# Value products ahead of the weight turns in every attention round

## The reference, cut to what matters

```
s = einsum('bchd,bkhd->bhck', q, k) * scale      # scores
s = where(allowed, s, -inf)
p = softmax(s, axis=-1)                          # weights
o = einsum('bhck,bkhd->bchd', p, v)              # value products
```

## Time and profile before

| | |
|---|---|
| median of the runs | 2584.94 us |
| the profiled execution | 2582.44 us |
| its span (first to last instruction) | 2580.6 us |
| PE busy | 2462.2 us, 95% of the span |
| DVE busy | 1743.6 us, 68% |
| ACT busy | 1078.4 us, 42% |
| mean granted TensorE clock | 0.987 of full speed |
| share of PE in the chain that ended last | 62% |

### The profile page before, as it was taken

One profiled execution on the slowest core, in us unless ns is written; L12 is line 12 of the kernel. 1 busy time (PEld: TensorE's weight loads), 2 busy tenths in 40 slices (PEclk: granted clock), 3 DMA queues, 4 the chain that ended last, 5 costly groups with the idle time before them and its releaser, 6 DMA issues.

```text
span 2580.6 us, 34583 instructions
## 1 busy us (share of the span) xinstructions
PE 2462.2 (95%) x13194; PEld 2051.7 (80%) x13194; DVE 1743.6 (68%) x2562; ACT 1078.4 (42%) x1846; POOL 361.4 (14%) x413
## 2 busy tenths in 40 slices
PE   3999999999999999999989999999999999999998
PEld 3678987779988878877648887888888888777997
DVE  6977886857995776776865474666575665345454
ACT  3466554556554212227645322224322224334443
POOL 1101111011111100104831110100100100000101
PEclk9999999999999999999989999999999999999999
DMA  8655885545773664553102263443363454322662
GB/s 302 215 175 188 294 312 198 194 156 208 253 265 124 201 198 139 188 180 91 62 20 82 98 196 131 154 180 103 106 213 117 153 189 123 100 72 66 188 196 90
DMA packets 135013, 420.92 MB, mean 163 GB/s; under 512 B 28352, under 2 KB 32576, under 8 KB 134848
## 3 DMA queue, kind: packets, MB, share of 16 engines
q1 hardware_dynamic: 134288, 416.98, 47.7%
q10 hardware_dynamic: 560, 1.72, 0.2%
HBM read 417.54 MB, written 1.11 MB: 162 GB/s over the span
## 4 chain that ended last, share of the span: by engine, by line
PE 62%; DVE 4%; ACT 2%; issue 1%; POOL 1%; DVEq 0%; POOLq 0%; ACTq 0%
PE ps L1123 19%; PE ps L1125 19%; PE ps L1124 19%; PE ps L1327 2%; PE ps L1276 1%; PE ps L1307 1%; DVE sl L1674 1%; DVE F L1792 1%; POOL ap L2185 1%; PE ps L1287 1%; DVE mjunk L1688 1%; ACT F L1449 1%; DVE ps L2029 0%; PE ps L1350 0%; PE ps L1224 0%
## 5 line engine op out<-in xcount | busy, mean ns | idle before, releaser
L1123 PE MATMUL ps<-hH,sh 128*128 128x256 f32 (+1 forms) x2560 | 840.5, 328 | 7.8 <-DVE hL L1763 3.5
L1125 PE MATMUL ps<-hH,sl 128*128 128x256 f32 (+1 forms) x2560 | 835.3, 326 | 0.0
L1124 PE MATMUL ps<-hL,sh 128*128 128x256 f32 (+1 forms) x2560 | 835.3, 326 | 0.0
L1390 ACT ACTIVATE sh<-raw 128x1024 fp32r<-128x1024 f32 x534 | 541.0, 1039 | 419.9 <-PE ps L1125 315.8
L1674 DVE TENSOR_TENSOR sl<-raw,sh 128x1024 fp32r<-128x1024 f32 x534 | 644.5, 1232 | 81.7 <-ACT sh L1390 81.0
L1688 DVE CUSTOM_DVE_ANT_0 mjunk<-raw,cB,V 128x1024 bf16<-128x1024 f32 x384 | 543.2, 1415 | 31.2 <-DMA C<-in_cst 8.5
L1123 PEld LDWEIGHTS ps<-hH,sh 128*128 128x128 f32 x2560 | 481.6, 188 | 60.6 <-issue 9.5
L1125 PEld LDWEIGHTS ps<-hH,sl 128*128 128x128 f32 x2560 | 482.0, 188 | 48.1
L1124 PEld LDWEIGHTS ps<-hL,sh 128*128 128x128 f32 x2560 | 481.0, 188 | 49.0 <-issue 1.7
L2158 POOL TENSOR_TENSOR uLl<-F,uHh 128x256 fp32r<-128x256 f32 (+1 forms) x132 | 163.0, 1235 | 1187.1 <-ACT uHh L1563 1089.8
L1123 PE MATMUL ps<-sh,uHh 128*128 128x512 f32 x792 | 313.2, 395 | 9.8 <-DVE sl L1674 9.6
(11 more groups left out here) (164 smaller groups left out, 2147.9 us busy)
## 6 DMA issues: line engine op xcount, KB each, us to landing
raw<-in_w SPq DMA_DIRECT2D x756, 512.0 KB, 4.6
G<-gates SPq DMA_DIRECT2D x14, 512.0 KB, 6.4
raw<-in_w SPq DMA_DIRECT2D x16, 256.0 KB, 4.1
cB<-in_rpb SPq DMA_DIRECT2D x64, 64.0 KB, 2.7
X<-in_x ACTq DMA_DIRECT2D x1, 1024.0 KB, 11.9
X<-in_ctx SPq DMA_DIRECT2D x1, 1024.0 KB, 7.9
out<-X SPq DMA_DIRECT2D x2, 512.0 KB, 3.1
raw<-in_w SPq DMA_DIRECT2D x2, 288.0 KB, 6.1
```

What stands on the lines that cost most here:

```text
L1123: self.e.matmul(out, lh, rh, start=start, stop=False)
L1124: self.e.matmul(out, lh, rl, start=False, stop=False)
L1125: return self.e.matmul(out, ll, rh, start=False, stop=stop)
L1390: self.e.activation(self.m["sh"][k % SPL][:, 0:w], self.m["raw"][r % RAW][:, 0:w], ACT.Copy).then_inc(self.sems["w_hi"], 1)
```

## The change

Inside a round, the step `att_o` of item k-4 (and `out`, when the row ends) is written ahead of `att_t` of item k-2. Nothing is added or removed.

```diff
@@ -379,10 +379,6 @@
                 self.add("att_e", st=st, it=it, i=k - 1)
                 if st["what"] == "na":
                     self.left(it["sc"])
-            if 0 <= k - 2 < n:
-                it = items[k - 2]
-                it["tb"] = self.bank()
-                self.add("att_t", st=st, it=it, i=k - 2)
             if 0 <= k - 4 < n:
                 it = items[k - 4]
                 if it["first"]:
@@ -391,6 +387,10 @@
                 self.add("att_o", st=st, it=it, i=k - 4)
                 if it["last"]:
                     st["out"](it, it["ob"])
+            if 0 <= k - 2 < n:
+                it = items[k - 2]
+                it["tb"] = self.bank()
+                self.add("att_t", st=st, it=it, i=k - 2)
```

## The result

| | before | after |
|---|---|---|
| median of 16 runs each, taken side by side | 2583.35 us | 2590.26 us |
| profiled execution | 2582.44 us | 2590.08 us |
| its span | 2580.6 us | 2588.3 us |
| mean granted TensorE clock | 0.987 | 0.986 |

The changed kernel is slower: ratio 1.0027, 95% interval 1.0018 to 1.0036, that is 6.9 us at these medians (4.7 to 9.3 by the interval). The forecast was 2590.7, from a sum of 5.8 us.

The account below looks back on a forecast made before the run. It took PE, busy 95%, as the bound, with DVE setting the pace around the moba rounds. Stalls of 2.74 + 2.19 + 0.9 = 5.8 us on the median 2584.94 gave 2590.7 us, range 2586 to 2595.

Parts of the forecast that it names:

- The covered waits: Exponential waits of turns in moba rounds 4 and 5: value products ahead gain 0 us, bound 1.1, as blocks wait for DVE.
- The bank in moba: Round 7: the turn gets the just-completed output bank and waits for DVE's division; 2.74 us later in layer 0, 2.19 in layer 1.
- dsa: Row end in both layers: the division wait stays, but one more turn comes late behind it; 0.45 us each, 0.9 us together.
- The clock: Rival, chance 0.24: PE's clock falls behind one or two of the four division stalls, 1.6 us a fall, to 2592.3 or 2593.9.
- The neighbourhood attention and the order inside PE: Neighbourhood bank waits: 0, bound 2.9 us; order of PE groups in 54 mixer and neighbourhood rounds: 0, bound 2.7 us.
- the pairing of the hand-overs: Between PE groups in a round followed by another: new order gives +0.09 and -0.09 us, which cancel.
- Part is given back: Rival, chance 0.22: delay shrinks at the fixed division after a low-clock block, by 1.6 us, or at later waits; about 2588 us.

Follow-up runs that it names:

- old_banks: The changed kernel's instruction order, with every bank asked for in the order of the kernel before; ratio 1.0001 to the kernel before.
- far_bank: Changed kernel, with the turn of the four mixer row-end rounds in another free bank and the rotation left as it was; ratio 1.0003 to the kernel before.
- filled_half: Changed kernel with four dummy products on PE inside each of the two new moba stalls; ratio 1.0042 to the kernel before.
- after_again: The changed kernel run once more, unchanged, for a second profile; ratio 1.0038 to the kernel before.
- mixer_only: Kernel before with the new order in the mixers' attentions only, the neighbourhood attention keeping its old order; ratio 1.0036 to the kernel before.
- before_again: The kernel before run once more, unchanged, for a second profile; its single run took 2583.95 us.
- neighbour_only: Kernel before with the new order in the neighbourhood attention only; ratio 1.0001 to the kernel before.
- keep_out: Changed kernel, with the output bank just completed in a round kept out of the choice for that round's turn; ratio 1.0037 to the kernel before.
- far_bank_before: Kernel before, with only dsa's turn of item 6 in another bank in each layer and the rotation unchanged; ratio 0.9991 to the kernel before.

## Why the prediction was right, and where only by luck

- *The covered waits (0)*: right. The delay at 137.4 is what it was at 92.9, to 0.02 us. What PE wins it waits again at the block, for DVE (1.20 became 1.59 in both layers). The turn's own wait in round 5 didn't fall by 0.4 each, as forecast, but from 0.91 to 0.80 and from 1.64 to 1.07: in layer 0 PE came 0.5 us earlier out of round 4 and waited that here too.
- *The bank in moba (2.74 and 2.19)*: right in place and size. The stall part is 2.74 in layer 0 when the block of round 5 runs at full clock (142.60 - 0.28 - 139.31 = 3.01, less the 0.27 by which the slow turn was longer, 0.77 against 0.50) and 2.09 in layer 1 (516.16 - 510.27 = 5.89, of which 3.80 were there at 508.4). old_banks and far_bank show that the bank causes it. What didn't hold is that DVE's time there is fixed: where the block of round 5 ran at the low clock the stall part was 2.0 in layer 0 too (filled_half), not 2.74.
- *dsa (0.9)*: 0.38 and 0.39, together 0.8. Right.
- *The clock (a rival with 0.24, 1.6 us a fall)*: this is the step that failed. I gave the clock to the smaller chance because stalls of 1.43 us had left it alone. It fell in both moba stalls, in all three kernels' profiles that have them unfilled (six of six: after, after_again, mixer_only, 1.88 to 2.45 us). The price of a fall was right for the stalls of 1.88: 3.59 - 2.01 = 1.6. Behind the longer one of layer 0 it is 5.26 - 2.74 = 2.5, in layer 1 3.58 - 2.09 = 1.5. Locally that is 4.0 us which the sum doesn't have. The timed runs agree in size: their mean granted clock is 0.9856 in the 22 of the changed kernel and 0.9873 in the 58 of before that have one on record. 0.0017 of 2588 us is 4 us, an estimate of what the clock costs in the total. The Trainium skill (TensorE: Matmul & The Clock Gate, "A second HAM failure mode: psum-queue depth-cycling") tells of a kernel whose PE idles between groups of matmuls often enough that its clock falls and rises again and again. The prediction took that as a rule for each single stall: the moba stalls agree with it, the dsa stalls of 1.82 us mostly don't (none in the six of after, after_again and mixer_only).
- *The neighbourhood attention and the order inside PE (0, bound 2.7)*: 0.90 to 1.00 us slower, within the bound. The step that failed is the pairing of the hand-overs: I had taken eight value products ahead of a turn at 0.84, from a place where no scores stood ahead of them, and a turn ahead of scores at 0.59. Behind scores the value products take 0.94 and the turn behind them 0.54; scores take 1.05 ahead of either group. So a round takes 2.53 against 2.47 or 2.48.
- *Part is given back (0.22)*: it is. From 159.0 to 444.9 both profiles of the changed kernel regain 1.74 us although dsa's 0.38 lies in that stretch, so 2.1 us come back; before_again loses 0.3 there. Most of it is before's fall at 410 to 420 us, 10 us at 0.83, which the changed kernel doesn't have. I had named another place, the block of round 5: both profiles of the changed kernel run it at full clock, and where it is slow (mixer_only, filled_half) 0.56 us are given back at the stall of layer 0, not the 1.6 of the forecast. Nor is it safely an effect of the change: neighbour_only, which is the kernel before up to there, hasn't that fall either. The stretch from 554.3 to 2219.4 is in no term: it differs by +1.76 and -1.32 us in the two profiles.

By the trace the sum is 2.74 + 2.09 + 0.8 + 0.9 = 6.5 us of waiting and order, 4.0 us of clock behind the stalls, and 2.1 back: 8.4 us. The two series measured 1.0027 and 1.0038, about 7 and 10 us. The forecast's place and the mechanism of the bank are right. Its sum of 5.8 came near because what it lacked, 4.9 us of clock and order, was partly paid by the 2.1 that came back, and because the spread of the measurement covers the rest. That part was luck. Open is what makes the clock fall at one place and not at another, and why the two kernels that kept it up at both stalls weren't faster.

## What to carry to other kernels

Where a planner hands out buffers in the order in which steps are written, moving a step moves every later buffer. Compare the bank numbers, not only the order, and look at each bank whose last reader has not begun. A fix that takes another bank without putting the rotation back moves the conflict elsewhere (keep_out: up to 4.8 us). Even where the rotation is put back, the bank that a step is given has a next user, and that one may wait in its place: 0.85 us in far_bank's moba, 0.89 us in far_bank_before. Before a wait is priced as a gain, look who writes that bank next and whose reading it would wait for.

## What the hardware showed beside that

At full granted clock, the same products run at two paces, in stretches of a hundred microseconds and more. Groups of L1125 (L1129) from 230 to 400 us, mean ns at the end, in before and in neighbour_only, whose instructions are the same there:

```profile
L1125 PE MATMUL ps<-hH,sl 128*128 128x256 f32 x342 | 94.4, 276 | 0.0
```
```profile
L1129 PE MATMUL ps<-hH,sl 128*128 128x256 f32 x342 | 96.2, 281 | 0.0
```

The starts tell more than these modelled lengths: from the turns at 222.02 (222.10) to the block at 412.79 (417.54) before takes 190.77 us and neighbour_only 195.44, with the clock at 1.00 in both up to 410. That is 4.7 us between two executions, for nothing that the kernel did, and it explains the 3.25 in its row of the table together with the fall at 410 that only before has. Before itself has 281 ns from 600 to 700 us and 276 from 780 to 830. Nothing in the runs says what sets the pace. A single profiled execution's span can so be off by as much as the effect that was measured here; the distance between two score groups can't.
